# Prompt attention of a one-core decoder step: projections moved between the blocks of the head before, and VectorE's division moved behind the next block's row maximum

## What is computed

```python
q = (_rms_norm(x @ wq_a, q_norm) @ wq_b).reshape(bsz, n, N_HEADS, QK_NOPE + QK_ROPE)
q_pe = _rope(q[..., QK_NOPE:], pos)
...
s = jnp.where(k_pos[None, :] <= qpos[:, None], s, -jnp.inf)
p = jax.nn.softmax(s, axis=-1).astype(ckv_new.dtype)
```

## Time and profile before

| | us |
|---|---|
| median of 3 runs | 2709.01 (2707.92 to 2711.21) |
| the profiled execution | 2707.35 |
| its span | 2705.5 |
| TensorE busy in the span | 2454.9 (91%) |
| VectorE, ScalarE, GpSimd busy | 1298.0 (48%), 773.7 (29%), 357.1 (13%) |

### The profile page before, as it was taken

How to read it: one execution, slowest core, us unless ns; L and a number is a source line. 1 busy time by engine, 2 the same in 40 slices (tenths; PEclk the granted TensorE clock), 3 DMA queues, 4 the chain that set the end, 5 groups by cost and what they waited for, 6 DMA issues and landing times.

```text
span 2705.5 us, 36839 instructions
## 1 busy us (share of the span) xinstructions
PE 2454.9 (91%) x14022; PEld 2228.9 (82%) x14022; DVE 1298.0 (48%) x2463; ACT 773.7 (29%) x1451; POOL 357.1 (13%) x288
## 2 busy tenths in 40 slices
PE   7899999999999777888887888899999999999994
PEld 7799999999998576777776666677989999999993
DVE  4523333333333755564565777745143333333336
ACT  2331111111111324444444555522311111111112
POOL 2400000000000600000003555314000000000006
PEclk9899999999999888998998999989999999999998
DMA  4121111111110121000002544440111111111111
GB/s 152 39 63 48 46 39 39 47 47 47 47 55 20 49 88 33 1 16 16 0 1 88 154 138 145 136 140 16 32 51 44 47 47 47 47 47 47 47 40 63
DMA packets 133769, 153.24 MB, mean 57 GB/s; under 512 B 10064, under 2 KB 109936, under 8 KB 133544
## 3 DMA queue, kind: packets, MB, share of 16 engines
q1 hardware_dynamic: 121392, 110.07, 13.1%
q0 software_dynamic: 12288, 41.95, 5.0%
HBM read 142.24 MB, written 10.32 MB: 56 GB/s over the span
## 4 chain that ended last, share of the span: by engine, by line
PE 75%; DVE 11%; issue 5%; ACT 5%; POOL 2%; DMA 2%; ACTq 0%; SPq 0%; POOLq 0%; DVEq 0%
PE ps L214 22%; PE ps L215 21%; PE ps L216 21%; DVE split L207 5%; ACT split L202 2%; PE ps L1776 2%; PE ps L1811 2%; DVE plain L290 1%; POOL plain L338 1%; POOL plain L340 1%; PE ps L222 1%; PE ps L221 1%; PE ps L1401 1%; PE ps L1791 1%; PE ps L1792 1%
## 5 line engine op out<-in xcount | busy, mean ns | idle before, releaser
L214 PE MATMUL ps<-split 128*128 128x344 f32 (+9 forms) x3632 | 1255.4, 346 | 106.9 <-DVE split L207 60.7
L215 PE MATMUL ps<-split 128*128 128x344 f32 (+9 forms) x3632 | 1237.1, 341 | 0.0
L216 PE MATMUL ps<-split 128*128 128x344 f32 (+9 forms) x3632 | 1236.1, 340 | 0.0
L214 PEld LDWEIGHTS ps<-split 128*128 128x128 f32 x3632 | 703.0, 194 | 164.8 <-issue 48.7
L216 PEld LDWEIGHTS ps<-split 128*128 128x128 f32 x3632 | 703.6, 194 | 38.0
L215 PEld LDWEIGHTS ps<-split 128*128 128x128 f32 x3632 | 703.8, 194 | 36.9
L202 ACT ACTIVATE split<-plain 128x344 fp32r<-128x344 f32 (+8 forms) x430 | 312.0, 758 | 646.7 <-PE ps L222 405.8
L207 DVE TENSOR_TENSOR split<-plain,split 128x1024 fp32r<-128x1024 f32 (+7 forms) x422 | 356.1, 867 | 196.5 <-ACT split L202 193.3
L274 DVE TENSOR_TENSOR plain<-plain,ps 128x512 f32<-128x512 f32 (+2 forms) x396 | 268.4, 685 | 202.3 <-PE ps L216 196.9
L207 DVE TENSOR_TENSOR split<-ps,split 128x512 fp32r<-128x512 f32 (+6 forms) x476 | 247.1, 558 | 203.9 <-ACT split L202 201.2
L910 DVE TENSOR_TENSOR plain<-plain,ps 128x350 f32<-128x350 f32 (+1 forms) x132 | 68.0, 515 | 567.8 <-ACT plain L866 567.2
(11 more groups left out here) (144 smaller groups left out, 1450.0 us busy)
## 6 DMA issues: line engine op xcount, KB each, us to landing
plain<-w_gate SPq DMA_DIRECT2D x44, 512.0 KB, 4.8
plain<-w_up SPq DMA_DIRECT2D x44, 512.0 KB, 4.0
plain<-w_down SPq DMA_DIRECT2D x44, 512.0 KB, 4.4
plain<-x_prompt SPq DMA_DIRECT2D x8, 512.0 KB, 11.4
x_spill<-plain SPq DMA_DIRECT2D x1, 4096.0 KB, 18.1
plain<-wo SPq DMA_DIRECT2D x8, 512.0 KB, 4.8
plain<-x_spill SPq DMA_DIRECT2D x8, 512.0 KB, 8.2
y_prompt<-plain SPq DMA_DIRECT2D x8, 512.0 KB
```

The source lines that it names most:

```text
L214: pe.matmul(out, still[0], moving[0], start=start, stop=False)
L215: pe.matmul(out, still[0], moving[1], start=False, stop=False)
L216: return pe.matmul(out, still[1], moving[0], start=False, stop=stop)
```

## The change

The hardware loops over pairs go. The stage becomes a prologue of twelve units (`PROLOGUE`: all units of head 0, and the first pair's values) and then one run over 64 blocks m, block n = m % 8 of head h = m // 8. The units of the next head stand between the blocks of this one, at three places of a block (`EARLY` behind the scores, `MID` and `LATE` around the last transposes), by two tables: `FOR_ODD` is used in even heads, and prepares the odd head behind and the rotary queries of the next pair; `FOR_EVEN` is used in odd heads. The number at the end of an entry is the PSUM bank. Value units take two blocks of rows. Weights are held and loaded per head (`wn`, `wk`) and per pair (`wr`, `wv`), and split in pieces of 256 to 512 columns at blocks 2 and 7 (`split_times`). On VectorE the order within a block is now row maximum, low parts, division; on ScalarE it is exponential, then high parts (with one exception in block 1).

```diff
+PROLOGUE = [("qp", 0, 0, 0), ("qp", 0, 1, 1), ("qn", 0, 0, 2), ("kn", 0, 0, 3), ("v", 0, 0, 4), ("qn", 0, 1, 6),
+            ("kn", 0, 1, 0), ("v", 0, 1, 1), ("kn", 0, 2, 2), ("v", 0, 2, 3), ("v", 0, 3, 4), ("v", 0, 4, 6)]
...
+FOR_ODD = {(1, MID): ("kn", 0, 4), (2, LATE): ("qn", 0, 4), (3, MID): ("kn", 2, 4), (3, LATE): ("kn", 1, 2),
+           (4, LATE): ("qn", 1, 2), (5, LATE): ("qp", 0, 2), (6, EARLY): ("qp", 1, 2)}
+FOR_EVEN = {(1, MID): ("kn", 0, 4), (1, LATE): ("qn", 0, 2), (2, EARLY): ("v", 0, 1), (3, EARLY): ("qn", 1, 4),
+            (3, LATE): ("kn", 1, 2), (4, LATE): ("v", 1, 2), (5, EARLY): ("v", 2, 2), (5, LATE): ("v", 3, 2),
+            (6, EARLY): ("kn", 2, 2)}
...
 def heads_pe(pe, k):
...
+        if i == 7 and h + 1 < k.heads:
+            if h % 2:
+                pe.wait_ge(s["hd_unit_lo"], k.unit_no["kn", h + 1, 2] + 1)
+            elif h + 2 < k.heads:
+                pe.wait_ge(s["hd_unit_lo"], k.unit_no["qp", h // 2 + 1, 1] + 1)
...
+    for m in range(8 * k.heads + 3):
+        h, n = m // 8, m % 8
+        if h < k.heads:
+            scores(h, n)
+            if h % 2 == 0 and n == 3:
+                sample_latent_queries(h // 2)
+        placed_unit(h, n, EARLY)
+        if n % 2 == 0 and m >= 4:
+            values((m - 4) // 2)
+        if 2 <= m < 8 * k.heads + 2:
+            turn(m - 2, 0)
+            turn(m - 2, 1)
+        placed_unit(h, n, MID)
+        if 2 <= m < 8 * k.heads + 2:
+            turn(m - 2, 2)
+        placed_unit(h, n, LATE)
+        if h < k.heads and h % 2 == 0 and n == 1:
+            sample_queries(h // 2)
...
 def heads_act(act, k):
...
+    def exp(m):
+        i = m % 8
+        pieces, w = score_pieces(k, i)
+        act.wait_ge(s["max_done"], m + 1)
+        if m >= 2:
+            act.wait_ge(s["filled"], FILLS_BEFORE[m - 1])
...
-            if 2 <= n < 18:
-                turned(j, n - 2)
-            if n < 16:
-                exp(j, n)
-            if n >= 4 and n % 2 == 0:
-                out(j, n - 3)
...
+        if n == 1 and turns:
+            turned(m - 2, 0)
+        if h < k.heads:
+            exp(m)
+        unit(unit_at(k, h, n, EARLY))
+        if n % 2 == 0 and m >= 4:
+            out((m - 4) // 2)
+        if turns:
+            if n != 1:
+                turned(m - 2, 0)
+            turned(m - 2, 1)
...
 def heads_dve(dve, k):
...
-            if 1 <= n < 17:
-                normalise(j, n - 1)
-            if n < 16:
-                row_max(j, n)
-            if n >= 2:
-                turned(j, n - 2)
...
+        if h < k.heads:
+            row_max(m)
+        if h < k.heads and h % 2 == 0 and n == 3:
+            sample_latent_queries(h // 2)
+        unit(unit_at(k, h, n, EARLY))
+        if turns:
+            turned(m - 2, 0)
+            turned(m - 2, 1)
+        if 1 <= m <= 8 * k.heads:
+            normalise(m - 1)
+        unit(unit_at(k, h, n, MID))
```

More of the change, by code:

```diff
@@ L1273, in heads_sp, with split_own @@
+    sp.wait_ge(s["own_w_lo"], 2 * k.heads)
     sp.wait_ge(s["sq_done"], k.heads)
     sp.wait_ge(s["sq_taken"], 6 * (k.heads // 2))
[L1277 to L1284, removed]
+def split_own(eng, k, h, act):
     s = k.s
-    for n, (raw, parts) in enumerate(((k.wq_raw, k.wq), (k.wkv_raw, k.wkv))):
+    for n, (raw, parts) in enumerate(((k.wn_raw(h), k.wn), (k.wk_raw(h), k.wk))):
@@ L1440, in heads_pe @@
-    pairs_of(pe, k, pair)
+        for n, (b, slot) in enumerate(slots):
+            if n == last_from:
+                pe.wait_ge(s["pt_lo"], RUNS_BEFORE[FILLS_BEFORE[m + 1]])
+            mm = product(pe, out, (v[:, 0, b, :], v[:, 1, b, :]), (k.pt[:, 0, slot, :], k.pt[:, 1, slot, :]),
+                         n == 0, n == len(slots) - 1)
+        mm.then_inc(s["pv_done"], 1)
+    for u in PROLOGUE:
+        n = k.unit_no[u[:3]]
+        if n >= 6:
+            pe.wait_ge(s["hd_unit_lo"], n - 5)
+        unit(*u)
@@ L1518, in heads_act @@
-    pairs_of(act, k, pair)
-def turned_view(k, g, n, place, slot, count):
-    cols = slice((n % 2) * P, (n % 2 + 1) * P)
+    act.wait_ge(s["extra_zero"], 8)
+    split_rotary(act, k, 0, True)
+    split_own(act, k, 0, True)
+    split_values(act, k, 0, True)
+    for u in PROLOGUE:
+        unit(u)
+        if u[:3] == ("kn", 0, 0):
+            rotary_query(0)
+    split_own(act, k, 1, True)
+    for m in range(8 * k.heads + 3):
+        h, n = m // 8, m % 8
+        turns = 2 <= m < 8 * k.heads + 2
+        if n == 1 and turns:
[11 more added lines that the diff above has]
+        if turns:
+            turned(m - 2, 2)
+        unit(unit_at(k, h, n, LATE))
+        if h < k.heads:
+            if n == 1 and h % 2 == 0:
+                sample_queries(h // 2)
+            if n == 1 and h + 1 < k.heads:
+                rotary_query(h + 1)
+            split_times(act, k, h, n, True)
@@ new lines, in unit @@
+            dve.tensor_tensor(rotated, rotated, k.swapped[t], ALU.add).then_inc(s["qp_steps"], 1)
+            return
+        if kind == "v":
+            before = value_ops_before(k, h, t)
+            parts = list(values_parts(k, h, t, bank))
+            dve.wait_ge(s["v_hi"], before + len(parts))
+            for n, (src, hi, lo) in enumerate(parts):
+                lo_part(dve, lo, src, hi).then_inc(s["v_lo"], 1)
+            dve.wait_ge(s["v_lo"], before + len(parts))
+            dve.sem_inc(s["hd_unit_lo"], 1)
+            return
```

590 lines of the change are left out of this document (361 added, 229 removed).

## The result

| | median, us | ratio to before | profiled span | granted clock |
|---|---|---|---|---|
| before | 2709.35 (2707.92 to 2711.21) | 1 | 2705.5 | 0.953 |
| after | 2770.51 (2762.89 to 2771.77) | 1.0219, interval 1.0200 to 1.0239 | 2767.7 | 0.949 |

A forecast was written before the change was run, and what follows sets the result against it. TensorE bounds it: 77 us of matmuls, 29 of waits and 1 of restarts make 107 per pair, with 7 of clock 114. The stage is 32 + 342 + 83 = 457, 37 us more: 2746 us, range 2716 to 2774.

The forecast's parts named there:

- The walk: One pair of heads followed block by block, each engine in its written order: TensorE's waits sum to 29 us against 17.
- scores(7) of the even head: TensorE's scores of block 7 need a bank that VectorE's rotary product releases: a wait of 4.5 us.
- exponential(6): ScalarE's exponential of block 6 starts only when block 4 is turned, at 6.3, though its maximum was there at 4.3.
- The clock: Slower TensorE clock after waits over 2.3 us: 7 us per pair, with bounds of 0 and 13.6.
- restarts: TensorE's stops and restarts at its waits: 1.3 us per pair.
- lead-in: Start of the stage to the scores of block 3 of the first pair, with twelve units: 32 us.
- tail: From block 3 of the last pair to the end of the stage, with few or no units: 83 us.
- I take nothing for code either way: Loops over pairs replaced by straight code: no cost or gain, as the last pair, already straight, took 100.2 us.
- the units cover everything: Rival: the serial round stays under TensorE's 4.8 us in nearly all blocks; 75 us less, 2634 us; chance 0.06.
- the exponential isn't held: Rival: exponential(m) does not wait for the turning of m-2; 4 us less, 2705 us; chance 0.08.
- the clock stays down: Rival: TensorE's clock falls at every wait, 13.6 us per pair or more; over 2774 us; chance 0.08.
- GpSimd's splits: GpSimd's weight splits, which stop VectorE's division: 5 us per pair in ten pieces, not two; cost left as it is.

The follow-up runs named there:

- hi_parts_first: The changed kernel with ScalarE's old order put back (high parts ahead of the exponential, early units ahead of both): 2682.29 us, ratio 0.9889 to before.
- after_shift128: The changed kernel with 128 satisfied waits put into TensorE's queue at the end of the decoding: 2759.46 us, ratio 1.0184 to before.
- three_buffers: The changed kernel with a third buffer for the probabilities of the first five heads, order of all engines unchanged: 2733.33 us, ratio 1.0090 to before.
- square of runs: Old and new engine order, each in the kernel before and in the pipeline over heads: pairs of 105.7 and 124.4 us before, 91.5 and 116.0 with the pipeline.
- best_both_shift79: The changed kernel with the old order of ScalarE and VectorE and 79 satisfied waits at the end of the decoding: 2664.28 us, ratio 0.9831 to before.
- division_first: The changed kernel with VectorE's old order put back (division, row maximum, low parts), ScalarE left alone: 2762.92 us, ratio 1.0181 to before.

## Why the prediction was right, and where its sizes were off

**The walk held.** These are the first six of TensorE's twelve waits in the pair from 1176.43, in order:

```profile
1182.05 0.39 PE L214 MATMUL ps<-split 128*128 128x328 f32 x1 [1.13 <-DVE split L207]
...
1195.44 0.50 PE L214 MATMUL ps<-split 128*128 128x512 f32 x1 [1.54 <-DVE plain L1728]
...
1204.68 0.66 PE L214 MATMUL ps<-split 128*128 128x352 f32 x1 [4.44 <-DVE plain L1728]
...
1213.59 0.58 PE L214 MATMUL ps<-split 128*128 128x256 f32 x1 [2.90 <-DVE split L207]
...
1223.47 0.90 PE L1550 MATMUL ps<-plain 128*128 128x128 f32 x3 [2.95 <-DVE plain L1797]
...
1237.24 0.39 PE L214 MATMUL ps<-split 128*128 128x264 f32 x1 [2.42 <-DVEq L1741]
```

Forecast for these six: 1.1, 1.6, 4.5, 2.6, 3.3, 2.7. The other six were forecast at 1.4, 0.9, 2.7, 2.4, 3.0 and 2.6 and are 1.2, 0.7, 2.6, 2.2, 2.9 and 2.3; one of 0.5, ahead of the turning of block 5, did not come. The sum was forecast at 29 and is 27.1. scores(7) of the even head waits for VectorE's rotary product as described, and exponential(6) ran 2.2 us behind its maximum, both as walked.

**The clock was sized too small, if its mean is the measure.** I took 7 us of a pair within bounds of 0 and 13.6; in the second and third pair it is (1 - 0.90) x 116.0 = 11.6. 77 + 27.1 + 11.6 = 115.7, and 117.0 with the 1.3 us of restarts in the forecast (a term that no run shows), against 116.0 measured. But the first pair has a clock of 0.93, 8.1 us by the same reckoning, and is just as long; its waits are 28.4 us. So part of the slower clock lies off the path, and how much isn't shown. What is sure is the time outside the waits: 77 + 1.3 + 7 = 85.3 us were forecast, 88.9 measured. With the waits 2 us shorter that is 2 us a pair over the forecast's 114. In sum the stage has 28.6 + 348.1 + 85.9 = 462.6 against 32 + 342 + 83 = 457: lead-in 3.4 less, pairs 6 more, tail 2.9 more. It starts 0.8 us sooner, not 2.2: TensorE's first unit still waits 2.9 us for GpSimd (5.0 before).

**"I take nothing for code either way"** is the step that failed. I looked at the stretch that was unrolled, which indeed runs no slower, and not at what stands behind it: unrolling moved the next loop against the blocks in which instructions are loaded. That was 12.5 us of the profiled run, a fifth of the loss. That 2770.5 lies in the range all the same, 3.5 under its upper end, is in part luck: that end was reckoned from the clock alone, and without the stops and the 6 us beside them the kernel would have come out near 2752. The Trainium skill (Runtime: NRT & Kernel Launch, "Instruction fetch mechanics") says that instructions come in blocks of 16 KiB, 256 of them, that TensorE's memory for them has 128 KiB, and that a taken branch whose target lies outside the current window of two pages forces a fetch. The runs agree on the blocks: packets of 16 KB, stops only where the loop goes back, gone after 128 instructions and back after 256. They don't agree on the window: the loop has 1624 instructions, over six blocks, and in the kernel before it goes back with no instruction packet between 2100 and 2450. Why it stays loaded at one place and not at another no run shows.

Of the last 6 us of the 62, 4 arise at the start of the output projection, where TensorE waits 3.5 us for low parts and 1.0 in the kernel before, and runs at half clock behind it:

```profile
1833.58 0.55 PE L214 MATMUL ps<-split 128*128 128x512 f32 x1 [3.53 <-DVE split L207]
```

That wait is 0.7 to 2.2 us in other traces with the same code there (0.7 in hi_parts_first, 2.2 in after_shift128), one trace each; its cause stays open. From the first matmul of the decoding to the last of the kernel, the stops and added waits taken off, the traces with this code give 1224 to 1234 us; before has 1227, after 1234.

**Rivals.** That the units cover everything (2634) was wrong for the order that was built; with the old one the kernel goes that way, to 2664. That the exponential isn't held fell by three_buffers, with pairs of 101 us where the forecast had put 102.5 without that wait. That the clock stays down (over 2774) came close: up to 11.6 of its 13.6 us. GpSimd's splits take 6.4 us a pair in six pieces, where 5 us in ten were forecast; they are not among the waits of a pair, so leaving their cost as it was was right as far as these runs tell.

What the prediction missed as an argument is that it priced the new order and the new structure together. Only the square of runs shows that the structure is a gain of 45 us (the stage takes 373.5 in best_both_shift79, 418.5 before) and the order a loss: 75 us by the medians in the kernel before, and 89 us of the stage in the pipeline (462.7 against 373.5).

## What to carry to other kernels

Before a step is put behind another on an engine's queue, close the chain into a ring (whose buffer or bank does the last step free for the first?) and compare one turn of it with the bound engine's time per step; here 5.1 us in the large blocks stood against 4.8 of TensorE's work in a block on average, and taking the link from exponential to high parts out was worth 3%. A change made of a new structure and a new order should be measured as a square of four, since the sum can hide a gain. And after unrolling or lengthening code, look at the issue stops and instruction packets of every loop behind it, not only of the part that was edited.

## What the runs showed of the hardware that I had not expected

- A loop that a kernel doesn't touch can be slowed by 4.4 us at a way back (6.3 with the clock behind it) when earlier code gets longer or shorter: 16 instruction packets in 350 us instead of none.
- A satisfied wait, an instruction of its own, is not free on TensorE: 128 in a row leave it idle for 9.7 us, 177 for 15.1 and 256 for 23.6. From 128 to 256 each costs 109 ns; the first 4 us (128 x 0.109 - 9.7) are hidden behind earlier matmuls, so 79 of them cost almost nothing where TensorE waited 4.9 us anyway (5.1 with them).
- The mean granted clock falls with the waits, but not by their sum alone: with 10 us of waits a pair had 0.98 (1.8 us by its length), with 17.3 it had 0.92 (8.5), with 27.1 0.90 (11.6) and with 32.0 0.89 (13.7 of 124.4), while three_buffers with 17.7 had 0.97 (3.0). Nor does all of it show in the time: two pairs of after at 0.93 and 0.90 both take 116.0 us, and the 2.3 us of waits that division_first saved gave back nothing.
